# A two-block transformer kernel: modulation sums moved to VectorE, an earlier convolution, and the second token half's attention placed behind the first queries

## What is computed

```python
# first block
proj = rms_norm(x) @ w_in                 # conv input, q, k, v, two gates
conv_o = silu(layer_norm(depthwise_conv31(a * sigmoid(gate)))) @ w_conv_out
attn_o = sliding_window_attention(q, k, v, sinks) @ w_attn_out
h = x + (sigmoid(gc) * conv_o + sigmoid(ga) * attn_o) @ w_out
h = h + hierarchical_moe(rms_norm(h))     # 32 experts, top 2 in one group
# second block
mod = silu(c) @ ada_w + ada_b             # 1024 x 6144 weights; six vectors:
sh1, sc1, g1, sh2, sc2, g2 = split(mod)   # shifts, scales, output gates
z = modulate(rmsnorm(h), sh1, sc1) @ w_in
out = (sig(ga) * attention(q, k, v) @ w_attn_out + sig(gh) * hyena(z) @ w_hy_out) @ w_out
x = h + g1 * out
q = modulate(rmsnorm(x), sh2, sc2) @ wq                  # 8 heads, two halves
eidx, g = top16 of 128 x 128 key pairs per head          # 128 picks a token
x = x + g2 * sum_k(gelu(u_tab[eidx_k] . x) * g_k * v_tab[eidx_k])
out = rmsnorm(x)
```

## Time and profile before

| | |
|---|---|
| median of three runs | 1729.56 us (1727.46 to 1732.55) |
| the profiled execution's own time | 1723.73 us |
| its span, first to last instruction | 1721.9 us |
| busy: PE, DVE, ACT, POOL | 1456.2, 885.1, 318.5, 503.7 us |
| HBM read | 563.49 MB, 328 GB/s over the span |

### The profile page before, as it was taken

One profiled execution on the slowest core, in us unless ns is written; L12 is line 12 of the kernel. 1 busy time (PEld: TensorE's weight loads), 2 busy tenths in 40 slices (PEclk: granted clock), 3 DMA queues, 4 the chain that ended last, 5 costly groups with the idle time before them and its releaser, 6 DMA issues.

```text
span 1721.9 us, 18101 instructions
## 1 busy us (share of the span) xinstructions
PE 1456.2 (85%) x6206; PEld 804.7 (47%) x6206; DVE 885.1 (51%) x1997; ACT 318.5 (18%) x643; POOL 503.7 (29%) x541
## 2 busy tenths in 40 slices
PE   7989989999999999999999874767767685867566
PEld 6866564444443434478878663222323232322222
DVE  3975152323232323465453988492938385744744
ACT  3124231101010101301052113111202021210001
POOL 3000000000000000000000555666666757575773
PEclk9999999999999999999999986787878788888789
DMA  9779729999999999943340978999999999999996
GB/s 314 277 278 337 293 99 382 427 428 429 429 428 429 429 428 428 381 147 125 120 135 1 343 295 317 360 394 379 350 409 330 404 340 391 337 392 349 379 370 251
DMA packets 135357, 565.40 MB, mean 328 GB/s; under 512 B 11513, under 2 KB 17446, under 8 KB 122748
## 3 DMA queue, kind: packets, MB, share of 16 engines
q1 hardware_dynamic: 60668, 295.66, 43.2%
q0 software_dynamic: 74416, 268.84, 40.8%
q10 hardware_dynamic: 208, 0.09, 0.0%
HBM read 563.49 MB, written 1.06 MB: 328 GB/s over the span
## 4 chain that ended last, share of the span: by engine, by line
PE 76%; issue 11%; DMA 5%; DVE 4%; POOL 3%; ACT 1%; another core or an unknown queue 0%; SPq 0%; POOLq 0%; DVEq 0%; ACTq 0%
PE psum L413 52%; PE psum L1044 22%; DMA ring<-in_peer_v_dram,attnT 2%; POOL ring L1194 2%; DVE arena L1645 1%; DMA ring<-in_peer_u_dram,attnT 1%; DMA ring<-in_w_in_dram 1%; PE psum L898 0%; DMA tok<-in_peer_v_dram,attnT 0%; PE psum L768 0%; PE psum L774 0%; DMA dft<-in_peer_v_dram,attnT 0%; POOL tok L1194 0%; DVE spec L1654 0%; PE psum L662 0%
## 5 line engine op out<-in xcount | busy, mean ns | idle before, releaser
L1044 PE MATMUL psum<-ring,arena 128*128 128x512 f32 x772 | 384.1, 647 | 180.3 <-DMA ring<-in_peer_v_dram,attnT 106.1
L1044 PEld LDWEIGHTS psum<-ring,arena 128*128 128x128 f32 x772 | 156.8, 206 | 404.7 <-issue 323.2
L413 PE MATMUL psum<-ring,arena 128*64 128x512 f32 (+1 forms) x1552 | 340.4, 594 | 1.4 <-DVE arena L1885 1.4
L2197 DVE CUSTOM_DVE_ANT_0 scratch<-ring,psum 128x1024 f32<-128x1024 f32 x216 | 255.5, 1219 | 68.6 <-DMA ring<-in_peer_u_dram,attnT 57.9
L413 PE MATMUL psum<-actT,ring 128*128 128x256 f32 (+1 forms) x1424 | 268.1, 349 | 21.6 <-issue 19.8
L1194 POOL DMA_INDIRECT dft<-in_peer_u_dram,attnT x10 | 9.9, 990 | 938.8 <-DVE attnT L2167 934.0
L413 PEld LDWEIGHTS psum<-actT,ring 128*128 128x128 f32 x1424 | 237.6, 197 | 52.3 <-issue 29.3
L1194 POOL DMA_INDIRECT ring<-in_peer_u_dram,attnT x216 | 205.9, 953 | 161.0 <-issue 63.9
L1194 POOL DMA_INDIRECT ring<-in_peer_v_dram,attnT x218 | 209.5, 961 | 70.1 <-issue 61.9
L413 PEld LDWEIGHTS psum<-ring,arena 128*64 128x64 f32 (+1 forms) x1552 | 109.2, 137 | 217.2 <-issue 203.8
L1495 ACT ACTIVATE arena<-ident,attnT 128x128 f32<-128x128 f32 x226 | 81.8, 396 | 412.5 <-PE psum L1044 183.6
(11 more groups left out here) (404 smaller groups left out, 1368.3 us busy)
## 6 DMA issues: line engine op xcount, KB each, us to landing
ring<-in_w_gate_dram SPq DMA_DIRECT2D x32, 2048.0 KB, 12.3
ring<-in_w_up_dram SPq DMA_DIRECT2D x32, 2048.0 KB, 16.5
ring<-in_w_down_dram SPq DMA_DIRECT2D x32, 2048.0 KB, 13.7
ring<-in_w_in_dram SPq DMA_DIRECT2D x15, 2048.0 KB, 14.7
ring<-in_ada_w_dram SPq DMA_DIRECT2D x12, 2048.0 KB, 11.7
ring<-in_w_out_dram SPq DMA_DIRECT2D x4, 2048.0 KB, 9.0
ring<-in_peer_wq_dram SPq DMA_DIRECT2D x4, 2048.0 KB, 15.1
ring<-in_w_attn_out_dram SPq DMA_DIRECT2D x2, 2048.0 KB, 11.8
```

What stands on the lines that cost most here:

```text
L413: return nc.tensor.matmul(o, lhsT, rhs, start=(k == 0), stop=(k == n - 1))
L1044: last = nc.tensor.matmul(psum[:, 4 + 2 * t + n, :], diag[:, i, :], rowbufs[b][:, n * 512:(n + 1) * 512], start=first, stop=final)
L2197: V.tensor_tensor_reduce(dotjunk[:, i % junk, :], rowbufs[b], x, 1.0, 0.0, ALU.mult, ALU.add, dots[:, t, k:k + 1]).then_inc(ev("dotted"), 1)
```

## The change

Groups 1 and 2 of the modulation weights are no longer multiplied on TensorE. VectorE multiplies each chunk by its column of silu(c) and adds it to `adasum` (`ada_step`), for group 2 all four pieces at once (2048 columns), for group 1 piece by piece (512 columns). TensorE then sums the 128 partitions with one matmul against ones a piece (`ada_sum`). Group 1 is loaded last, behind `wo1`; slots 3, 4, 5 and 0 go to the experts when `ada_summed` says so. The sine reductions are cut apart so that the convolution starts after the second, and ten taps of its second half precede the filter products. `gate_unit(.., 0, 3)` moves behind the transposes of the convolution.

In the second mixer, pairs 4 to 7 of attention (t = 1) lose their place ahead of the first output projection: their transposes and products follow the first queries. With them go the t = 1 merges. The probabilities get rooms of their own (`prob_rooms`); ring slots 0 and 4 change places in `rowbufs`, and `ROW_ORDER` and `room_reader` follow. All 512 gathers remain.

```diff
-        mtmp = {"a": arena1[:, 0:1024].rearrange("p (b c) -> p b c", b=2)}
+        mtmp = {"a": scratch}
+        adasum = arena1[:, 0:2048].rearrange("p (g n) -> p g n", n=512)
...
+        prob_rooms = [arena2[:, 0:1024], arena2[:, 1024:2048], arena2[:, 2048:3072], arena2[:, 3072:4096],
+                      arena1[:, 3072:4096], arena2[:, 1024:2048], arena2[:, 2048:3072], arena2[:, 3072:4096]]
+        prob2 = [room[:, 512 * r:512 * (r + 1)] for room in prob_rooms for r in range(2)]
...
-        rowbufs += [ring[:, 4, r * D:(r + 1) * D] for r in range(4)] + [ring[:, 0, r * D:(r + 1) * D] for r in range(4)]
+        rowbufs += [ring[:, 0, r * D:(r + 1) * D] for r in range(4)] + [ring[:, 4, r * D:(r + 1) * D] for r in range(4)]
...
-        ROW_ORDER = [*range(10), *range(4), 10, 11, *range(4, 8), *range(12, 20), *range(8, 12), *range(0, 6), *range(20, 24), *range(6, 10), *range(12, 16), *range(24, 28)]
+        ROW_ORDER = [*range(10), *range(7), 10, 11, *range(7, 10), *range(12, 20), *range(7), 10, 11, *range(7, 10), *range(20, 24), *range(12, 16), *range(24, 28)]
...
-        pieces += ada_of[0] + [("o0", A["w_conv_out"][0].rearrange("(k p) n -> p k n", p=P))] + ada_of[1]
+        pieces += ada_of[0] + [("o0", A["w_conv_out"][0].rearrange("(k p) n -> p k n", p=P))]
         pieces += [("g10", kpiece(w_in, g0 + D)), ("g11", kpiece(w_in, g0 + D + 512))]
         pieces += ada_of[2]
         pieces += [("o1", A["w_attn_out"][0].rearrange("(k p) n -> p k n", p=P)),
                    ("wo0", kpiece(A["w_out"][0], 0)), ("wo1", kpiece(A["w_out"][0], 512))]
+        pieces += ada_of[1]
...
+            def ada_sum(p, summed):
+                pe.wait_ge(ev("ada_summed"), summed)
+                b = groups[f"mr{p}"][0] if p == GATE_ROWS else bank(f"mr{p}")
+                for g in range(4):
+                    last = nc.tensor.matmul(psum[32 * g:32 * g + 1, b, :], ones[:, 0:1], adasum[:, g, :], start=p != GATE_ROWS, stop=True)
+                last.then_inc(bank_full[b], 1)
...
-            for i in range(4):
+            for i in range(3):
...
-            emptied(pe, "prm")
-            ada_rows(0)
+            gate_unit(place1, "a", 0, 3)
...
+            emptied(pe, "prm")
+            ada_rows(0)
...
-            ada_rows(1)
-            gate_unit(place1, "a", 1, 0)
-            ada_columns(1)
-            abs_columns()
-            for i in range(1, 4):
+            for i in range(4):
                 gate_unit(place1, "a", 1, i)
+                if i == 0:
+                    abs_columns()
...
-                    ada_gate_step(h)
...
+            ada_sum(GATE_ROWS, 1)
...
+            ada_sum(1, 2)
...
+            ada_columns(1)
...
-            for i in range(len(pairs)):
-                if i + 2 < len(pairs):
-                    score2(i + 2)
+            for i in range(4):
+                score2(i + 2)
                 pt2(i)
                 if i:
                     pv2(i - 1)
-                if i < 4:
-                    mixed_half(1, 1, 0, (6,), (i,))
-                if i == 5:
-                    landed(place2, "o0")
-                    emptied(pe, "pw0")
-                    mixed_half(0, 0, 0, (6,))
-                if i == 6:
-                    mixed_half(0, 0, 1, (0,))
-            pv2(len(pairs) - 1)
-            everyday.append((7, 1, 2, 3, 4, 5, 6, 0))
+            pv2(3)
+            score2(6)
+            landed(place2, "o0")
+            emptied(pe, "pw0")
+            mixed_half(0, 0, 0, (6,))
+            mixed_half(0, 0, 1, (7,))
+            score2(7)
+            everyday.append((5, 4))
             pe.wait_ge(ev("bmerged"), 1)
             out_unit_rows(place2, "b", 0, 0)
             out_unit_rows(place2, "b", 0, 1)
-            emptied(pe, "pw1")
-            mixed_half(0, 1, 0)
+            mixed_half(1, 1, 0, (6,))
...
-            mixed_half(0, 1, 1)
+            mixed_half(1, 1, 1, (7,))
...
+            pt2(4)
             queries(0, 0, "b", (2, 3))
-            mixed_half(1, 1, 1)
+            pv2(4)
+            pt2(5)
             key_scores(0, 0, "b", (2, 3), ("b",))
+            pv2(5)
+            for i in (6, 7):
+                pt2(i)
+                pv2(i)
+            emptied(pe, "pw1")
+            mixed_half(0, 1, 0)
+            mixed_half(0, 1, 1)
             queries(1, 0, "a", (0, 1))
+            queries(1, 0, "b", (2, 3))
+            key_scores(0, 1, need=("a", "b"))
...
+            def used_up(name):
+                on_vector = {f"ada{j}": turn for turn, p in enumerate((GATE_ROWS, 1)) for j in ada_groups[p]}
+                if name in on_vector:
+                    sp.wait_ge(ev("ada_summed"), on_vector[name] + 1)
+                else:
+                    filled(last_reader[name])
...
-            for s in (1, 2, 3, 4, 5, 0):
-                if s == 5:
-                    sp.wait_ge(ev("amerged"), 1)
-                    sp.dma_start(ctxw, kpiece(w_in2, CH, 2 * KV * HD)).then_inc(ev("ctxw_in"), 16)
+            sp.wait_ge(ev("amerged"), 1)
+            sp.dma_start(ctxw, kpiece(w_in2, CH, 2 * KV * HD)).then_inc(ev("ctxw_in"), 16)
+            for s in (1, 0, 3, 2, 4, 5):
                 prev = [nm for i, (nm, _) in enumerate(pieces) if i % SLOTS == s][-1]
-                filled(last_reader[prev])
+                used_up(prev)
...
-            room_reader = {2: "bo011", 6: "bo111", 10: "bx11", 12: "pq01", 16: "pq11", 20: "pq21", 24: "pq31"}
+            room_reader = {2: "bo111", 6: "bo011", 10: "bx11", 12: "pq01", 16: "pq11", 20: "pq21", 24: "pq31"}
...
+            sine_args(0)
             v(V.memset(vpad[:, :, 0:30], 0.0))
-            conv_half(0)
+            sine_args(1)
+            conv_start(0)
+            conv_taps(0, 0, 6)
+            sine_args(2)
+            conv_taps(0, 6, TAPS)
+            conv_start(1)
+            conv_taps(1, 0, 10)
...
-            conv_half(1)
+            conv_taps(1, 10, TAPS)
...
+            def ada_step(p, k, slots, g0, done=False):
+                if k == 0:
+                    for s in slots:
+                        name = [nm for nm, _ in pieces if place1[nm][0] == s and nm in [f"ada{j}" for j in ada_groups[p]]][0]
+                        dve.wait_ge(piece_in[s], 16 * place1[name][1])
+                acc = adasum[:, g0:g0 + len(slots), :]
+                w = ring[:, slots[0]:slots[-1] + 1, k * 512:(k + 1) * 512]
+                if k == 0:
+                    v(V.tensor_scalar(acc, w, scT[:, k, 0:1], None, ALU.mult))
+                else:
+                    v(V.scalar_tensor_tensor(acc, w, scT[:, k, 0:1], acc, ALU.mult, ALU.add), "ada_summed" if done else None)
...
+                if t:
+                    ada_step(GATE_ROWS, 0, (2, 3, 4, 5), 0)
+                    ada_step(GATE_ROWS, 1, (2, 3, 4, 5), 0)
...
+            for k in range(2, KD):
+                ada_step(GATE_ROWS, k, (2, 3, 4, 5), 0, k == KD - 1)
...
+            def ada_piece(g, s, k0, k1):
+                for k in range(k0, k1):
+                    ada_step(1, k, (s,), g, g == 3 and k == KD - 1)
+            full(dve, f"mr{GATE_ROWS}")
+            ada_piece(0, 3, 0, KD)
+            ada_piece(1, 4, 0, KD)
             add_in(0, 0)
+            ada_piece(2, 5, 0, 3)
             add_in(0, 1)
             v(V.tensor_copy(stat("dummy", 1), epscol[:, 0:1]), "ah_ready")
+            ada_piece(2, 5, 3, 5)
             rn_rows(0)
+            ada_piece(2, 5, 5, KD)
+            ada_piece(3, 0, 0, KD)
...
             best_of(0, (0,), "0a")
             rows_of_table(0, (0,))
-            merge_half(1, 1, 1, True)
             best_of(0, (1,), "0b")
             rows_of_table(0, (1,))
             shift_of(0)
+            full(dve, "pw1")
+            dots_of(0, range(0, 3), 1)
+            merge_half(0, 1, 0, True)
+            merge_half(0, 1, 1, True)
+            dots_of(0, range(3, 7), 1)
+            picks_of(1)
             mix_in(1, 0)
-            dots_of(0, range(0, 4), 1)
             mix_in(1, 1)
-            dots_of(0, range(4, 5), 1)
+            dots_of(0, range(7, 9), 1)
             pn_rows(1)
-            dots_of(0, range(5, 8), 1)
+            dots_of(0, range(9, 11), 1)
             half_out("pn", 1, modsc[:, 2, :], mod[:, 24:32, 0])
-            picks_of(1)
-            dots_of(0, range(8, GROUP))
+            dots_of(0, range(11, GROUP))
             weigh(0)
```

142 lines of the change are left out of this document (71 added, 71 removed).

## The result

| | before | changed |
|---|---|---|
| median of five runs | 1729.41 us (1727.46 to 1732.55) | 1738.02 us (1736.65 to 1745.32) |
| span of the profiled execution | 1721.9 us | 1735.4 us |
| busy: PE, DVE, POOL | 1456.2, 885.1, 503.7 us | 1446.1, 924.2, 501.9 us |

The ratio is 1.0054, 95% interval 1.0035 to 1.0072. The forecast was 11 us faster, 1718.5 us.

A forecast was written before the change was run, and what follows sets the result against it. TensorE bounds the experts; the table stage has DMA share 0.94. Preparation -18.5 and second mixer +7.5 make -11: 1723.73 profiled becomes 1712.7, median 1718.5 us; range 1706 to 1731.

The forecast's parts named there:

- the convolution's 6.3 us: Preparation: convolution fills VectorE's idle time, so its transposes on TensorE come some 6.3 us earlier, at about 90.2.
- attend1: Preparation, TensorE: eight modulation steps leave the first attention, cutting first transposes to projection from 15.4 to 8.2 us, -7.2.
- VectorE's steps: Preparation: VectorE's modulation steps run from 141 to 204.5, with TensorE never waiting for them.
- gives its lead back: Second mixer: TensorE's 10.4 us lead at the first output projection is lost; query blocks start 10.5 us later.
- gather 51 carries to the end: Table stage: the last query block sets gather 51, near 1035.5; from there to the end 675 us as before.
- (d): Preparation, TensorE: two added sums, about 1.04 us each, placed where it waits anyway; cost nothing, or 1 us.
- VectorE's last piece: Preparation: group 1's last piece ends at about 204.5, delaying only add_in(1, 0), whose half is needed by 207.5.
- the longer order: Second mixer: attention pairs, projections, queries and picks in their new order make the query blocks start 10.5 us later.
- `picks_of(1)` ahead of `mix_in(1, 0)`: Second mixer: VectorE is in these picks to 976, while TensorE has the t = 1 result by 974.4.
- the stretches: Under the gathers TensorE's rows thin out with no semaphore awaited, 12.4 and 9.3 us before; taken for late instructions.
- two stretches of unbroken gathers: Gathers 27 to 42 and 43 to 50 again stall TensorE's last query blocks; +7.5 is left of 10.5.
- two more stretches: Slower rival: 25 us more stalls between 939 and 986, beside attention's small matmuls; +14, 1743 us; chance 0.09.

The follow-up runs named there:

- prep_fixed: prep_only with VectorE's last group 1 steps behind the normed t = 0 half's outputs and TensorE's second sum behind t = 1's routing product; ratio 0.9934.
- prep_fixed2: prep_fixed with the group 1 sum, its copy and its transposes moved further back; ratio 0.9904 to the kernel before.
- after_window3: The changed kernel with at most three gathers in flight for the first 51; ratio 0.9958 to the kernel before.
- window3: prep_fixed2 with at most three gathers in flight instead of six for gathers 28 to 51; ratio 0.9862 to the kernel before.
- quiet runs: Four kernels run in surroundings where the kernel before takes 1649.91 us and none of the four traces shows the stretches.
- picks_late: The changed kernel with picks_of(1) moved back behind the residual, norm and outputs of t = 1; ratio 0.9966, among the quiet runs.
- held: The changed kernel with gathers 7 to 17 held until the key scores of queries(1, 0) are done; ratio 1.0070 to the kernel before.
- gate_later: prep_fixed with rooms 16 to 19 released by pq21 instead of pq11; ratio 0.9943 to the kernel before.
- window4: prep_fixed2 with at most four gathers in flight for gathers 28 to 51; ratio 0.9813 to the kernel before.
- prep_only: The kernel before with only the change's preparation part (modulation sums, convolution, order of loads); ratio 0.9946, among the quiet runs.

## Why the prediction was wrong

**Right:** the convolution's 6.3 us (transposes at 90.40; 90.2 foretold), `attend1` (7.5 us from its first transposes to the projection, 8.2 foretold), VectorE's steps, from 141.4 to 206.8 (141 to 204.5), never late for TensorE's sums; the loads; that TensorE gives its lead back in front of the last query blocks; the rounds unchanged; and that gather 51 carries to the end (13.2 us there, 13.5 at the end).

**Wrong, the preparation, 7 us** (18.5 foretold, 11.4 measured): the step was (d), two sums that cost "Nothing, or 1 us", and the sentence that VectorE's last piece delays only what isn't needed yet. It delayed the outputs of the first half, which stood behind it on VectorE's list, and TensorE waited 2.41 us; I had followed `add_in(1, 0)` and not the next instruction. The second sum took 1.88 us with nothing to cover it. Behind that, ScalarE's copy of the sums stood ahead of sixteen context outputs on which TensorE waits. prep_fixed and prep_fixed2 show both: with all of it moved back, the experts start at 235.9 to 241.4.

**Right in size, the longer order, 11 us:** I had 10.5. Without stretches the new order costs 11.8 (after_window3's 780.0 against window3's 768.2), and 10.0 in the quiet runs (779.3 against 769.3). So nearly half of the 24.5 us is the order itself. The prediction named `picks_of(1)` ahead of `mix_in(1, 0)` as the step that TensorE waits for; picks_late shows that this place is worth only 2 to 3 us of it. What makes up the rest wasn't taken apart.

**Wrong, the stretches, 16 us:** the step was "in the new order there are two stretches of unbroken gathers again", with 7.5 of the 10.5 left, so 3 us fewer of stretches. Stretches cost 24.4 us before (792.6 less 768.2) and 37.1 in the changed kernel (817.1 less 780.0), 12.7 more.

For the two that I had walked, the working holds. The 192 and 128 rows of the last query blocks, with the key scores between them, take 24.2 us more before than in window3, and 23.0 more in the changed kernel than in after_window3. All of the rest lies in front of them. Counted from the experts' first matmul, the changed kernel begins these rows 14.2 us later than after_window3 does (999.84 - 242.32 against 988.43 - 245.07). Of that the gaps at 929 and 952 are 11.3 (4.23 and 9.50 us, where after_window3 waits 1.82 and 0.58). Another 4.7 are slower rows behind the gaps: the projections at 936.27 take 8.86 us instead of 7.41, `out_unit_rows` 15.41 instead of 13.90, and two short groups the rest. No gather runs beside `out_unit_rows` there; the granted clock does it, 0.50 from 961.7 to 966.0. A shorter wait for VectorE (6.65 against 8.36) gives 1.7 back.

So I let the moved attention and the queries behind it run free of stretches, and gave two more stretches there a chance of 0.09. That case had the mechanism, at 25 us instead of 14. In hindsight the trace held a warning: its two stretches lay where many short instructions ran beside unbroken gathers, and the change puts attention's last products, 64 projection rows and 64 query rows into such a place.

**Shown and not shown.** Shown, by held, gate_later, window3, window4 and after_window3: the stretches need gathers issued without a pause, and go when fewer are in flight; and the last two begin at fixed places in the code. Full DMA engines alone don't make one: before 1000 us in the kernel before, and in prep_only, TensorE ran on at a share of 0.98 to 0.99. That it is the fetching of instructions is an inference. For it: the fixed places; that VectorE's picks in held and ScalarE's copy are late as well; that TensorE's long rows are spared; and that the profile shows no semaphore awaited by TensorE. No run shows an instruction transfer arriving late. The Trainium skill, "Runtime: NRT & Kernel Launch", section "Instruction fetch mechanics", calls the cost of the next block mostly hidden; if the inference is right, that holds in the quiet runs and in window3, and not in the rows of the changed kernel above. Against a plain lack of DMA time stands this view of prep_only, DMA queues between 940 and 1075 us, a quiet run:

```profile
q0 software_dynamic: 13164, 47.97, 91.6%
q1 hardware_dynamic: 2080, 4.19, 8.1%
q8 instruction: 5, 0.08, 0.2%
q14 instruction: 6, 0.05, 0.1%
```

There are 11 instruction transfers, where the earlier trace rows has 9; gathers and loads keep the engines busier (99.7% against 79.4% before), and there is no stretch. Why the quiet runs differ in this isn't settled.

## What to carry to other kernels

Before you move short instructions beside a saturating stream of transfers, look in the trace for single rows with idle time that no semaphore explains. If they are there, leave the stream small gaps (fewer transfers in flight) and measure again, since the slower stream can make the whole faster. Count the slow clock behind each gap into its price. An earlier start of a stream is worth nothing where a later gate on another engine sets its end: follow the gates. When work is put onto an engine "with idle time", check what stands next on its list, not only the instruction whose bank it fills, and do the same on the engine that reads the result.
